# RWKV chunk products in four 64x64 quadrants of TensorE, and two preparation passes moved from VectorE to ScalarE

## Chip, cores, metric

One core of a Trainium2 chip runs one program. The metric is the device time in microseconds of one execution, the median of several.

## The reference, cut to what matters

Two layers; in each, a feed-forward half-step, a mixer of three branches on 512 tokens of 1024 features, a second feed-forward half-step and a gated embedding. The change touches only the RWKV branch: 8 heads of width 64, chunks of 64 tokens, all in float32. Per chunk and head it computes

```python
lhs = jnp.eye(RW_CHUNK, dtype=f32) - L_ab                    # unit lower triangular
W1 = triangular_solve(lhs, a_dec)
U0 = triangular_solve(lhs, L_ak @ v)
Q_eff = r_dec + M_rb @ W1
Y_intra = M_rb @ U0 + M_rk @ v
P = W1.T @ b_dec + exp(g_last) * eye(n)
D = U0.T @ b_dec + v.T @ k_dec
S_next = S @ P + D                                            # over the 8 chunks, in order
y = Y_intra + Q_eff @ S.T
```

before which the decays are cumulated and exponentiated, `kk = k * k_k` is divided by its norm over the head, and `k = k * (1 + (a - 1) * k_a)`.

## The kernel before

**Dense products.** Every large product runs through one helper (`open_group`, L848). Weights come by DMA on SP's queue into a ring of three slots; POOL splits each into a high and a low half (L1169, L1172), and TensorE multiplies three combinations of 128x128 by 128x512.

**The RWKV cores.** Heads are taken in pairs: core `ft` (0 to 3) handles two heads of 64 features, four token tiles of 128 tokens, each of two chunks (`cp` 0 and 1, in partitions 0 to 63 and 64 to 127). `rwkv_core_pe` issues for one core, in this order on TensorE: the pair products (L388), transposes to token-major (L379), then six levels that widen the inverse of `lhs` from blocks of 1 to 64. A level is the strips (L402), which VectorE masks into `xl` (L697), then the widening of `inv` (L414), which VectorE adds (L730), and that of `invT` (L420), which VectorE adds (L735). Each of these is 16 products of 64x64 by 64x64 and leaves 32 records, since a float32 product is two passes. Then the solution (L484, 16 products with 128 columns), which ScalarE copies to `xx` (L1581); the products for P and Q (L498, L502) and D (L508, L512), four passes of 16; the part of y inside the chunk (L524, L528); and a loop over chunks 1 to 7 that needs the previous state (L544, L550; VectorE adds at L750).

Between these, `advance(n)` issues n blocks of a dense product (three matmuls of 512 columns each): the numbers stand in `FILL_MANY` (cores 0 and 1), `FILL_FEW` (core 2) and `FILL_LAST` (core 3). PSUM banks come from `take`: the bank used longest ago, 3 to 7 for cores 0 and 1 and 4 to 7 for cores 2 and 3; TensorE waits there for the step that frees the bank's last user.

**VectorE and ScalarE.** Each has one instruction order, written out. While core `ft` runs, VectorE also prepares core `ft + 1`: `prepare_dve` is a generator, and `core_dve` takes steps from it by `aside(n)` at fixed places: one before the bonus, two after each strip of levels 2 to 5, two after each `invT` update, one before P and Q are added (L743), one per chunk of the state loop. From its step 12 on they are: `kk` (L590), the cumulation (L594), `rw_csm` (L597), the two operations on `k` (L604, L608), L613, the maximum of the key norms (L616), then L624, L626, L631, the scaling of `kk` by the inverse norm (L635), L639, L641, L644, L647, L652, L654. ScalarE's inverse norm is `norms_keys` (a table load, Ln at L1421, a table load, Exp at L1422); it stands in ScalarE's order behind the copies of D (L1585). `norm_squares` (L1393) and `decays` (L1399 to L1402) stand before the copy of the solution.

```python
            aside(1)

            now("rw_kept", L, ft)
            for cp in range(2):
                now("rwpq_done", L, ft, cp)
```

Of the kernel before, what the change touches and what calls it, by code (L numbers as in the profile page):

```python
# [28 lines left out]
P = 128  # L29
# [33 lines left out]
R_LNG, R_LNB, R_MU, R_W0, R_A0, R_KK, R_KA, R_RK, R_LB, R_HN, R_GNG, R_GNB = 0, 32, 64, 79, 83, 87, 91, 95, 99, 107, 111, 115  # L63
# [74 lines left out]
def build(nc, a, out, counts, banks_of):  # L138
# [4 lines left out]
    with ctx:  # L143
# [175 lines left out]

        def bank_units(b):  # L320
            return b[:, :].rearrange("p (u n) -> p u n", n=HEAD)
# [42 lines left out]
        def rwkv_core_pe(pe, take_bank, used_last, advance, L, ft):  # L364
# [3 lines left out]
            UNITS = [(hd, t) for t in range(NT) for hd in range(2)]  # L368
# [7 lines left out]
            def token_major(i, src):  # L376
                b = take(("rwt", L, ft, i), ("rw_tok", L, ft, i))
                for t in range(NT):
                    ins = nc.tensor.transpose(b[:, t * P:(t + 1) * P], src(t), ident())  # L379
                ins.then_inc(*step("rwt_done", L, ft, i))  # L380
# [11 lines left out]

            def strips(lev):
                b = take(("rwx", L, ft, lev), ("rw_x", L, ft, lev) if lev else ("rw_inv", L, ft, 0))
                if lev == 0:
                    for hd in range(2):
                        pe.wait_ge(*after("rw_mask", L, ft, 0, hd))
                else:
                    pe.wait_ge(*after("rw_inv", L, ft, lev - 1))
                for hd, t in UNITS:  # L400
                    for cp in range(2):
                        ins = nc.tensor.matmul(b[unit(cp), unit_cols(hd, t)], bm[unit(cp), hd, t, 0, :],  # L402
                                               ident()[unit(cp), unit(cp)] if lev == 0 else inv[unit(cp), NT * hd + t, :],
                                               start=True, stop=True)
                ins.then_inc(*step("rwx_done", L, ft, lev))

            def widen(lev):
                pe.wait_ge(*after("rw_x", L, ft, lev))
                pe.wait_ge(*after("rw_invT", L, ft, lev - 1))
                if lev < top:  # L410
                    b = take(("rwi", L, ft, lev), ("rw_inv", L, ft, lev))
                    for hd, t in UNITS:
                        for cp in range(2):
                            ins = nc.tensor.matmul(b[unit(cp), unit_cols(hd, t)], invT[unit(cp), NT * hd + t, :],  # L414
                                                   xl[unit(cp), NT * hd + t, :], start=True, stop=True)
                    ins.then_inc(*step("rwi_done", L, ft, lev))
                b = take(("rwj", L, ft, lev), ("rw_invT", L, ft, lev))
                for hd, t in UNITS:
                    for cp in range(2):
                        ins = nc.tensor.matmul(b[unit(cp), unit_cols(hd, t)], xl[unit(cp), NT * hd + t, :],  # L420
                                               invT[unit(cp), NT * hd + t, :], start=True, stop=True)
# [8 lines left out]
            strips(0)  # L430
# [3 lines left out]
            token_major(1, lambda t: ar[:, t, 0, :])  # L434
# [15 lines left out]
            for lev in range(2, top + 1):  # L450
# [4 lines left out]
                if lev == 2:  # L455
# [4 lines left out]
                    b = take(("rwl", L, ft), ("rw_lakv", L, ft))  # L460
                    for hd, t in UNITS:
                        for cp in range(2):
                            ins = nc.tensor.matmul(b[unit(cp), unit_cols(hd, t)], km[unit(cp), hd, t, 0, :],
                                                   v_tok[unit(cp), ft % 2, t, unit(hd)], start=True, stop=True)
# [12 lines left out]
            pe.wait_ge(*after("rw_lakv", L, ft))  # L477
            pe.wait_ge(*after("rw_tok", L, ft, 1))
            pe.wait_ge(*after("rw_invT", L, ft, top))
            for hd in range(2):  # L480
                b = take(("rwu", L, ft, hd), ("rw_wu", L, ft, hd))
                for t in range(NT):
                    for cp in range(2):
                        ins = nc.tensor.matmul(b[unit(cp), t * P:(t + 1) * P], invT[unit(cp), NT * hd + t, :], rhs[unit(cp), hd, t, :],  # L484
                                               start=True, stop=True)
                ins.then_inc(*step("rwu_done", L, ft, hd))
# [7 lines left out]
            for hd in range(2):  # L494
                pe.wait_ge(*after("rw_wu", L, ft, hd))
                for t in range(NT):
                    for cp in range(2):
                        nc.tensor.matmul(pq_bank[cp][unit(hd), t * HEAD:(t + 1) * HEAD], xx[unit(cp), hd, t, 0:HEAD],  # L498
                                         b_tok[unit(cp), t, unit(hd)], start=True, stop=True)
                for t in range(NT):  # L500
                    for cp in range(2):
                        ins = nc.tensor.matmul(pq_bank[cp][unit(hd), 256 + t * HEAD:256 + (t + 1) * HEAD], xx[unit(cp), hd, t, 0:HEAD],  # L502
                                               bm[unit(cp), hd, t, 1, :], start=True, stop=True)
                        if hd and t == NT - 1:
                            ins.then_inc(*step("rwpq_done", L, ft, cp))
                for t in range(NT):
                    for cp in range(2):
                        nc.tensor.matmul(d_bank[cp][unit(hd), t * HEAD:(t + 1) * HEAD], b_tok[unit(cp), t, unit(hd)],  # L508
                                         xx[unit(cp), hd, t, HEAD:P], start=t == 0, stop=False, skip_group_check=True)
                for t in range(NT):  # L510
                    for cp in range(2):
                        ins = nc.tensor.matmul(d_bank[cp][unit(hd), t * HEAD:(t + 1) * HEAD], k_tok[unit(cp), t, unit(hd)],  # L512
                                               v_tok[unit(cp), ft % 2, t, unit(hd)], start=False, stop=t == NT - 1,
                                               skip_group_check=True)
                        if hd and t == NT - 1:
                            ins.then_inc(*step("rwd_done", L, ft, cp))
# [51 lines left out]
        def prepare_dve(v, now, chain, L, ft):  # L568
# [21 lines left out]
            v.tensor_scalar(rw_kk[:, :], rkv[:, 1, :], parT[:, R_KK + ft:R_KK + ft + 1], None, ALU.mult).then_inc(*step("rw_kkr", L, ft))  # L590
            yield

# [14 lines left out]
            now("rw_made", L, ft, "ka")  # L607
            v.scalar_tensor_tensor(rw_k2[:, :], rw_k2[:, :], 1.0, rkv[:, 1, :], ALU.add, ALU.mult).then_inc(*step("rw_k2", L, ft))  # L608
# [606 lines left out]
        def _(act):  # L1215
# [174 lines left out]
            def norm_squares(L, ft):  # L1390

                now("rw_kkr", L, ft)
                nc.scalar.activation(rw_ss[:, :], rw_kk[:, :], ACT.Square).then_inc(*step("rw_sq", L, ft))  # L1393
# [616 lines left out]
```

## Time and profile before

| what | value |
|---|---|
| runs of before | 3162.68, 3166.0, 3166.46 us, median 3166.0 us |
| the profiled execution | 3162.28 us, its span 3160.2 us |
| mean granted TensorE clock | 0.984 |
| TensorE matmul busy | 3018.1 us (96%), 20178 records |
| VectorE busy | 1380.2 us (44%), 1779 instructions |
| ScalarE busy | 628.4 us (20%), 1023 instructions |
| GpSimd busy | 2350.3 us (74%), 1877 instructions |

Busy is the union of the instructions' times; a matmul's end is modelled and its records overlap, so the distance from one start to the next tells what a product costs. All times in rows are us from the span's start, unless ns is written. The eight cores run from 682.5 to about 891 us (layer 0) and from 2249.4 to about 2459 us (layer 1).

### The profile page before, as it was taken

How to read it: one execution, taken by the hardware profiler on the slowest of the kernel's cores; microseconds unless marked ns; L12 is line 12 of the kernel's file. 1: busy time of each engine (PE TensorE's matmuls, PEld its weight loads, DVE VectorE, ACT ScalarE, POOL GpSimd, SP SyncE). 2: the span in 40 equal slices, each digit the busy share in tenths (PEclk: the TensorE clock that was granted, in tenths of full speed). 3: DMA queues.
4: the chain of work that ended last, by engine and by line, in shares of the span. 5: the costliest groups of instructions: out<-in, count | busy, mean ns of one | idle time of the engine just before them, and what ended most of it. 6: DMA issues, size and time to landing. Idle time of an engine off the chain costs nothing. (4 is left out here: it accounts for less than half of the span.)

```text
span 3160.2 us, 47691 instructions
## 1 busy us (share of the span) xinstructions
PE 3018.1 (96%) x20178; PEld 2460.4 (78%) x20178; DVE 1380.2 (44%) x1779; ACT 628.4 (20%) x1023; POOL 2350.3 (74%) x1877
## 2 busy tenths in 40 slices
PE   8999999889989999999899999998999899999996
PEld 7888877677768888888788888776777688888884
DVE  4221333766636563211852214248665375622127
ACT  1000125443310020000310002354432100200011
POOL 8988786743249989888899888867331599898875
PEclk9999999999989999999999999999999899999998
DMA  4332332111013333323233223321110133333322
GB/s 138 100 100 94 100 120 61 43 44 39 29 41 94 126 95 106 100 94 100 87 94 107 94 100 107 105 57 47 40 46 16 54 94 126 100 107 94 100 87 87
DMA packets 201488, 266.60 MB, mean 84 GB/s; under 512 B 12305, under 2 KB 130429, under 8 KB 201277
## 3 DMA queue, kind: packets, MB, share of 16 engines
q1 hardware_dynamic: 194624, 243.51, 25.3%
q10 hardware_dynamic: 6652, 20.05, 1.7%
q8 instruction: 160, 2.62, 0.3%
q14 instruction: 52, 0.42, 0.0%
HBM read 257.22 MB, written 6.29 MB: 83 GB/s over the span
## 5 line engine op out<-in xcount | busy, mean ns | idle before, releaser
L1169 POOL TENSOR_TENSOR w_hi<-w_raw,zero 128x512 fp32r<-128x512 f32 (+2 forms) x936 | 1088.3, 1163 | 703.4 <-PE ps L848 661.8
L1172 POOL TENSOR_TENSOR w_lo<-w_raw,w_hi 128x512 fp32r<-128x512 f32 (+2 forms) x936 | 1288.5, 1377 | 73.5
L848 PE MATMUL ps<-hT_hi,w_hi 128*128 128x512 f32 (+1 forms) x2368 | 933.7, 394 | 35.7 <-DVE y_raw L793 15.6
L848 PE MATMUL ps<-hT_hi,w_lo 128*128 128x512 f32 (+1 forms) x2368 | 909.3, 384 | 0.0
L848 PE MATMUL ps<-hT_lo,w_hi 128*128 128x512 f32 (+1 forms) x2368 | 908.8, 384 | 0.0
L848 PEld LDWEIGHTS ps<-hT_hi,w_hi 128*128 128x128 f32 x2368 | 446.3, 188 | 148.2 <-POOL w_lo L1172 22.5
L848 PEld LDWEIGHTS ps<-hT_hi,w_lo 128*128 128x128 f32 x2368 | 445.7, 188 | 89.5
L848 PEld LDWEIGHTS ps<-hT_lo,w_hi 128*128 128x128 f32 x2368 | 446.9, 189 | 84.6 <-issue 2.9
L1723 DVE TENSOR_TENSOR act_raw<-silu,ps 128x512 f32<-128x512 f32 x88 | 59.9, 681 | 616.9 <-PE ps L848 616.9
L848 PE MATMUL ps<-w_hi,aT_hi 128*128 128x512 f32 x704 | 274.7, 390 | 0.0
L848 PE MATMUL ps<-w_lo,aT_hi 128*128 128x512 f32 x704 | 274.1, 389 | 0.0
L848 PE MATMUL ps<-w_hi,aT_lo 128*128 128x512 f32 x704 | 274.0, 389 | 0.0
L1312 ACT ACTIVATE silu<-ps 128x512 f32<-128x512 f32 x88 | 52.7, 598 | 883.6 <-PE ps L848 880.0
L1743 DVE SCALAR_TENSOR_TENSOR h_tok<-ps,h_tok 128x512 f32<-128x512 f32 x48 | 32.8, 683 | 437.3 <-PE ps L848 437.3
L848 PEld LDWEIGHTS ps<-w_lo,aT_hi 128*128 128x128 f32 x704 | 132.2, 188 | 27.5
L848 PEld LDWEIGHTS ps<-w_hi,aT_hi 128*128 128x128 f32 x704 | 132.2, 188 | 27.2
L848 PEld LDWEIGHTS ps<-w_hi,aT_lo 128*128 128x128 f32 x704 | 132.2, 188 | 27.2
L848 PE MATMUL ps<-w_hi,hT_hi 128*128 128x512 f32 x320 | 128.8, 402 | 3.4 <-POOL w_lo L1172 2.4
L1727 DVE TENSOR_TENSOR aT_lo<-act_raw,aT_hi 128x512 fp32r<-128x512 f32 x88 | 129.1, 1467 | 3.0
L848 PE MATMUL ps<-w_lo,hT_hi 128*128 128x512 f32 x320 | 124.9, 390 | 0.0
L848 PE MATMUL ps<-w_hi,hT_lo 128*128 128x512 f32 x320 | 124.8, 390 | 0.0
L1269 ACT ACTIVATE ln_rstd<-ln_mv,ln_eps 128x1 f32<-128x1 f32 x32 | 9.5, 297 | 441.6 <-DVE ln_mv L1686 441.6
(303 smaller groups left out, 3558.3 us busy)
## 6 DMA issues: line engine op xcount, KB each, us to landing
w_raw<-in_w_in SPq DMA_DIRECT2D x104, 512.0 KB, 3.6
w_raw<-in_ffn_wg SPq DMA_DIRECT2D x176, 256.0 KB, 2.8
w_raw<-in_ffn_wu SPq DMA_DIRECT2D x176, 256.0 KB, 3.1
w_raw<-in_ffn_wd SPq DMA_DIRECT2D x88, 512.0 KB, 3.6
w_raw<-in_w_in SPq DMA_DIRECT2D x96, 128.0 KB, 2.3
w_raw<-in_w_out SPq DMA_DIRECT2D x16, 512.0 KB, 3.8
w_raw<-in_ple_gate SPq DMA_DIRECT2D x16, 512.0 KB, 3.7
ln_rows<-in_ln_g ACTq DMA_DIRECT2D x8, 512.0 KB, 4.0
```

Source lines behind the costliest of these rows:

```text
L848: ins = nc.tensor.matmul(o, l_, r_, start=first, stop=last, skip_group_check=into is not None)
L1169: nc.gpsimd.tensor_tensor(w_split[0][:, q, kk, 0:w], w_raw[:, r, kk, 0:w], zero[:, 0:1].to_broadcast([P, w]), ALU.add).then_inc(*step("w_h ...
L1172: nc.gpsimd.tensor_tensor(w_split[1][:, q, kk, 0:w], w_raw[:, r, kk, 0:w], w_split[0][:, q, kk, 0:w].bitcast(F32), ALU.subtract).then_inc( ...
L1269: nc.scalar.activation(ln_rstd[:, t, :], ln_mv[:, t, 1:2], ACT.Sqrt, bias=ln_eps[:, :]).then_inc(*step("ln_sqrt", L, q, t))
L1312: nc.scalar.activation(silu[:, m, :], b[:, :], ACT.Silu).then_inc(*step("silu_done", L, f, g, m))
L1723: v.tensor_tensor(act_raw[:, m, :], silu[:, m, :], b[:, :], ALU.mult).then_inc(*step("act_raw", L, f, g, m))
L1727: v.tensor_tensor(aT[1][:, k, :], act_raw[:, m, :], aT[0][:, k, :].bitcast(F32), ALU.subtract).then_inc(*step("act_rest", L, f, k))
L1743: v.scalar_tensor_tensor(z, b[:, :], 0.5 if name == "down" else 1.0, z, ALU.mult, ALU.add).then_inc(*step("res_sum", L, q, half, m))
```

## The change

`PLACES` replaces `UNITS`: for odd token tiles the row half and the output half of a product differ (`side = cp ^ (t % 2)`), so that even tiles use the two quadrants on the diagonal and odd tiles the two others. Even and odd tiles write to two PSUM banks. `xl`, `invT` and the right-hand side of odd tiles lie in the other partition half than their chunk. This holds for the strips of levels 1 to 5, the widening of `inv`, the product of `km` with v and the solution. The widening of `invT` stays within halves. At level 0 the crossed copy of odd tiles is made by 8 more products into a bank of its own (`rwc`), and the transposes of `ar` for odd tiles become two products of 64 output partitions each. P, Q and D are reordered to `corners`, and both waits for `xx` now stand before them. VectorE's masks and additions on `xl` and `inv` are split in two by parity. `kk = k * k_k` is no longer made beforehand: ScalarE squares with a scale, and VectorE multiplies k by `k_k` where it scales by the inverse norm. `1 + (a - 1) * k_a` is made by one ScalarE instruction in `decays`. So two steps of `prepare_dve` fall away. The diff, cut:

```diff
+            PLACES = [(hd, t, cp, cp ^ (t % 2)) for hd in range(2) for t in range(NT) for cp in range(2)]
...
             def strips(lev):
-                b = take(("rwx", L, ft, lev), ("rw_x", L, ft, lev) if lev else ("rw_inv", L, ft, 0))
...
+                b = two_banks("rwx", "rw_x", lev)
+                pe.wait_ge(*after("rw_inv", L, ft, lev - 1, 1))
+                for hd, t, cp, side in PLACES:
+                    ins = nc.tensor.matmul(b[t % 2][unit(side), parity_cols(hd, t)], bm[unit(cp), hd, t, 0, :],
+                                           inv[unit(cp), NT * hd + t, :], start=True, stop=True)
...
             def widen(lev):
...
+                    b = two_banks("rwi", "rw_inv", lev)
+                    for hd, t, cp, side in PLACES:
+                        ins = nc.tensor.matmul(b[t % 2][unit(cp), parity_cols(hd, t)], invT[unit(side), NT * hd + t, :],
+                                               xl[unit(side), NT * hd + t, :], start=True, stop=True)
...
+                for hd, t, cp, side in PLACES:
+                    u = NT * hd + t
+                    ins = nc.tensor.matmul(b[unit(cp), HEAD * u:HEAD * u + HEAD], xl[unit(cp), u, :], invT[unit(cp), u, :],
+                                           start=True, stop=True)
...
+            b = [take(("rwu", L, ft, odd), ("rw_wu", L, ft, odd)) for odd in range(2)]
+            last = {}
+            for hd, t, cp, side in PLACES:
+                c = P * (2 * hd + t // 2)
+                last[t % 2] = nc.tensor.matmul(b[t % 2][unit(cp), c:c + P], invT[unit(side), NT * hd + t, :],
+                                               rhs[unit(side), hd, t, :], start=True, stop=True)
+            for odd in range(2):
+                last[odd].then_inc(*step("rwu_done", L, ft, odd))
...
+            for odd in range(2):
+                pe.wait_ge(*after("rw_wu", L, ft, odd))
+            corners = ((0, 0), (1, 1), (0, 1), (1, 0))
+            for t in range(NT):
+                for cp, hd in corners:
+                    nc.tensor.matmul(pq_bank[cp][unit(hd), t * HEAD:(t + 1) * HEAD], xx[unit(cp), hd, t, 0:HEAD],
+                                     b_tok[unit(cp), t, unit(hd)], start=True, stop=True)
...
-            v.tensor_scalar(rw_kk[:, :], rkv[:, 1, :], parT[:, R_KK + ft:R_KK + ft + 1], None, ALU.mult).then_inc(*step("rw_kkr", L, ft))
-            yield
...
-            now("rw_a", L, ft)
-            now("rw_csm", L, ft)
+            now("rw_ka", L, ft)
             if ft:
                 now("rwb_done", L, ft - 1)
-            v.tensor_scalar(rw_k2[:, :], rw_a[:, :], 1.0, parT[:, R_KA + ft:R_KA + ft + 1], ALU.subtract, ALU.mult).then_inc(
-                *step("rw_made", L, ft, "ka"))
-            yield
...
-            v.scalar_tensor_tensor(rw_kk[:, :], rw_kk[:, :], SS_SCALE ** 0.5, rw_ss[:, :], ALU.mult, ALU.mult).then_inc(
+            v.scalar_tensor_tensor(rw_kk[:, :], rkv[:, 1, :], parT[:, R_KKS + ft:R_KKS + ft + 1], rw_ss[:, :], ALU.mult, ALU.mult).then_inc(
...
+                nc.scalar.activation(rw_ss[:, :], rkv[:, 1, :], ACT.Square, scale=parT[:, R_KK + ft:R_KK + ft + 1]).then_inc(*step("rw_sq", L, ft))
...
             def decays(L, ft):
                 now("rw_csm", L, ft)
+                now("par_more", L)
+                nc.scalar.activation(rw_k2[:, :], rw_a[:, :], ACT.Identity, bias=parT[:, R_KA1 + ft:R_KA1 + ft + 1],
+                                     scale=parT[:, R_KA + ft:R_KA + ft + 1]).then_inc(*step("rw_ka", L, ft))
```

The `aside` counts stay as they are, so every later step of `prepare_dve` moves to a place two earlier. On VectorE, in core 1 of a layer, from the last strips to the first state, before:

```order
L697 TENSOR_TENSOR xl<-ps,cons 128x8x32 [waits rwx_done]
L608 SCALAR_TENSOR_TENSOR rw_sw<-rw_sw,rkv 128x512 [waits rw_made]
L613 TENSOR_TENSOR rw_keep<-rkv,rw_sw 128x512 [waits rw_k2]
L735 TENSOR_TENSOR invT<-invT,ps 128x8x32 [waits rw_invT,rwj_done]
L616 TENSOR_SCALAR rw_ss<-ps 128x512 [waits rwss_done]
L624 TENSOR_TENSOR ar<-rkv,rw_e 128x4x128 [waits rwm_done,rwt_done,rw_e3]
L626 TENSOR_TENSOR k_inv<-rw_sw,rw_cs 128x512
L743 TENSOR_TENSOR pq<-ps,pq_add 128x8x64 [waits rwpq_done,rw_kept]
L743 TENSOR_TENSOR pq<-ps,pq_add 128x8x64 [waits rwpq_done]
L750 TENSOR_TENSOR rhs<-ps,rhs 128x64 [waits rws_done,rw_d]
```

and now:

```order
L717 TENSOR_TENSOR xl<-ps,cons 128x4x32 [waits rwx_done]
L717 TENSOR_TENSOR xl<-ps,cons 128x4x32
L635 TENSOR_SCALAR rw_ss<-ps 128x512 [waits rwss_done]
L643 TENSOR_TENSOR ar<-rkv,rw_e 128x4x128 [waits rwm_done,rwt_done,rw_e3]
L760 TENSOR_TENSOR invT<-invT,ps 128x8x32 [waits rw_invT,rwj_done]
L645 TENSOR_TENSOR k_inv<-rw_sw,rw_cs 128x512
L650 TENSOR_TENSOR rw_dec<-k_inv,rw_e 128x512 [waits rw_made]
L654 SCALAR_TENSOR_TENSOR rw_kk<-rkv,parT,rw_ss 128x512 [waits rw_rn]
L768 TENSOR_TENSOR pq<-ps,pq_add 128x8x64 [waits rwpq_done,rw_kept]
L768 TENSOR_TENSOR pq<-ps,pq_add 128x8x64 [waits rwpq_done]
L775 TENSOR_TENSOR rhs<-ps,rhs 128x64 [waits rws_done,rw_d]
```

The maximum of the key norms now stands ahead of the last `invT` update, and the scaling of `kk`, which waits for ScalarE's `rw_rn`, ahead of both additions of P and Q; before, both stood behind.

On TensorE in the changed kernel, core 1, from P to the part of y inside the chunk (it is L498 to L528 of the kernel before, and waits there for the same two names):

```order
L525 MATMUL ps<-b_tok,xx 64x64 x15
L529 MATMUL ps<-bm,xx 64x64 x16
L535 MATMUL ps<-xx,b_tok 64x64 x16
L539 MATMUL ps<-v_tok,k_tok 64x64 x16
L551 MATMUL ps<-xx,bm 64x64 [waits rw_pq,rw_wu]
L551 MATMUL ps<-xx,bm 64x64 x7
```

The part of y waits for `rw_pq` because `take` gives it the bank from which VectorE adds P and Q.

On VectorE in the changed kernel, before core 0, from the end of the cumulation on:

```order
L621 TENSOR_TENSOR rw_e<-rw_cs,rw_sw 128x512 [waits rw_made]
L627 TENSOR_TENSOR rw_sw<-rw_sw,rkv 128x512 [waits rw_ka]
L1953 TENSOR_TENSOR y_raw<-ps,hg_g 128x512 [waits hg_in,hg_osq]
L632 TENSOR_TENSOR rw_keep<-rkv,rw_sw 128x512 [waits hgo_done,rw_k2]
L1953 TENSOR_TENSOR y_raw<-ps,hg_g 128x512 [waits hg_in,hg_osq]
L635 TENSOR_SCALAR rw_ss<-ps 128x512 [waits rwss_done]
L1953 TENSOR_TENSOR y_raw<-ps,hg_g 128x512 [waits hg_in,hg_osq]
L643 TENSOR_TENSOR ar<-rkv,rw_e 128x4x128 [waits rw_e3]
L1953 TENSOR_TENSOR y_raw<-ps,hg_g 128x512 [waits hg_in,hg_osq]
```

Before, all four products of the HGRN branch (L1918) stood ahead of the maximum of the key norms; now two of them stand behind it.

## Rows read from the trace of the kernel before

**Rows 1.** Page, busy time of each engine: TensorE.

```profile
PE 3018.1 (96%) x20178; PEld 2460.4 (78%) x20178; DVE 1380.2 (44%) x1779; ACT 628.4 (20%) x1023; POOL 2350.3 (74%) x1877
```

**Rows 2.** Windows: start:end, length, busy time (and instructions) of each engine, granted clock, DMA.

```profile
2249.40:2361.60 112.20, 111.16 (x1920) 87.37 (x1920) 69.99 (x127) 43.08 (x72) 33.00 (x28) 0.98 0.12 32
```

**Rows 3.** Timeline of TensorE, core 1 of layer 1: start, us, line, what, [idle before].

```profile
2315.48 1.10 PE L402 MATMUL ps<-inv,bm 64*64 64x64 f32 x32
2316.41 1.10 PE L463 MATMUL ps<-v_tok,km 64*64 64x64 f32 x32
```

**Rows 4.** Groups by line and form: strips; busy us, mean ns, idle before.

```profile
L402 PE MATMUL ps<-inv,bm 64*64 64x64 f32 x1280 | 44.5, 219 | 3.6 <-DVE inv L711 3.0 <-DVE inv L730 0.5
```

**Rows 5.** Timeline of TensorE: pair products in four quadrants, 128 columns.

```profile
2305.25 1.10 PE L388 MATMUL ps<-ar,b_inv 64*64 64x128 f32 x32
2306.29 1.21 PE L379 MATMUL ps<-cons,rw_dec 128*128 128x128 f32 x8
```

**Rows 6.** Timeline of TensorE, core 0 of layer 1: where L512 and L498 meet.

```profile
2290.89 0.22 PE L498 MATMUL ps<-b_tok,xx 64*64 64x64 f32 x1
2290.90 0.22 PE L512 MATMUL ps<-v_tok,k_tok 64*64 64x64 f32 x1
2290.90 0.22 PE L498 MATMUL ps<-b_tok,xx 64*64 64x64 f32 x1
2290.95 0.22 PE L512 MATMUL ps<-v_tok,k_tok 64*64 64x64 f32 x1
```

**Rows 7.** Timeline of TensorE, core 1 of layer 1: from the solution to y.

```profile
2341.57 1.97 PE L484 MATMUL ps<-rhs,invT 64*64 64x128 f32 x32
2343.47 0.50 PE L848 MATMUL ps<-hT_hi,w_hi 128*128 128x512 f32 x1
...
2345.06 0.68 PE L498 MATMUL ps<-b_tok,xx 64*64 64x64 f32 x16
...
2348.84 0.68 PE L524 MATMUL ps<-xx,bm 64*64 64x64 f32 x16
...
2350.85 0.50 PE L848 MATMUL ps<-hT_hi,w_hi 128*128 128x512 f32 x1
```

**Rows 8.** Timeline of ScalarE, the same stretch.

```profile
2342.71 0.60 ACT L1581 ACTIVATE xx<-ps 128x512 f32<-128x512 f32 x1 [5.38 <-PE ps L484]
...
2348.87 0.66 ACT L1585 ACTIVATE rhs<-ps 128x256 f32<-128x256 f32 x2 [4.68 <-PE ps L512]
...
2352.78 0.63 ACT L1422 ACTIVATE rw_ss<-rw_ss 128x512 f32<-128x512 f32 x1
```

**Rows 9.** Timeline of VectorE, core 1 of layer 1.

```profile
2314.76 0.42 DVE L730 TENSOR_TENSOR inv<-inv,ps 128x256 f32<-128x256 f32 x1 [0.40 <-PE ps L414]
...
2340.29 0.69 DVE L616 TENSOR_SCALAR rw_ss<-ps 128x512 f32<-128x512 f32 x1 [0.62 <-PE ps L348]
...
2348.00 1.29 DVE L743 TENSOR_TENSOR pq<-ps,pq_add 128x512 f32<-128x512 f32 x2 [4.98 <-PE ps L502]
...
2354.24 1.28 DVE L635 SCALAR_TENSOR_TENSOR rw_kk<-rw_kk,rw_ss 128x512 f32<-128x512 f32 x1
```

**Rows 10.** Timeline of TensorE: waits before core 0 and in core 2, layer 1.

```profile
2249.40 0.92 PE L388 MATMUL ps<-ar,b_inv 64*64 64x128 f32 x12 [6.39 <-issue]
...
2363.65 0.55 PE L379 MATMUL ps<-cons,rw_dec 128*128 128x128 f32 x3 [0.86 <-DVE yt L765]
...
2403.45 0.68 PE L524 MATMUL ps<-xx,bm 64*64 64x64 f32 x15 [0.60 <-DVE pq L743]
```

**Rows 11.** Windows behind the wait before core 0, columns as in rows 2.

```profile
2249.40:2253.10 3.70, 3.70 (x41) 3.37 (x42) 2.62 (x6) 0.60 (x1) 0.00 (x0) 0.50 0.34 96
...
2253.20:2257.00 3.80, 3.79 (x100) 3.13 (x99) 2.11 (x4) 0.60 (x1) 0.00 (x0) 1.00 0.02 4
```

**Rows 12.** Timelines before and in core 0: VectorE, ScalarE.

```profile
2233.08 0.69 DVE L1918 TENSOR_TENSOR y_raw<-ps,hg_g 128x512 f32<-128x512 f32 x1 [0.41 <-ACT y_raw L1544]
...
2279.67 1.27 ACT L1416 ACTIVATE y_raw<-ps,parT 128x512 f32<-128x512 f32 x2 [4.26 <-PE ps L447]
```

More of the change, by code:

```diff
@@ L391, in pairs, with two_banks @@
                     last[hd].then_inc(*step("rwm_done", L, ft, i, hd))
-            def strips(lev):
-                b = take(("rwx", L, ft, lev), ("rw_x", L, ft, lev) if lev else ("rw_inv", L, ft, 0))
[L395 to L404, printed above, removed]
+            def two_banks(name, freed, lev):
+                return [take((name, L, ft, lev, odd), (freed, L, ft, lev, odd)) for odd in range(2)]
@@ new lines, in first_strips @@
+            def first_strips():
+                b = take(("rwx", L, ft, 0, 0), ("rw_inv", L, ft, 0, 1))
+                b2 = take(("rwc", L, ft), ("rw_invT", L, ft, 0))
+                for hd in range(2):
+                    pe.wait_ge(*after("rw_mask", L, ft, 0, hd))
+                for hd, t, cp, side in PLACES:
+                    eye = ident()[unit(cp), unit(cp)]
+                    u = HEAD * (NT * hd + t)
+                    ins = nc.tensor.matmul(b[unit(cp), u:u + HEAD], bm[unit(cp), hd, t, 0, :], eye, start=True, stop=True)
+                    if t % 2:
+                        ins = nc.tensor.matmul(b2[unit(side), parity_cols(hd, t)], eye, bm[unit(cp), hd, t, 0, :],
+                                               start=True, stop=True)
+                ins.then_inc(*step("rwx_done", L, ft, 0))
@@ L429, in rwkv_core_pe @@
             advance(fill["pairs"])
-            strips(0)
+            first_strips()
             pairs(1, k_inv)
@@ L459, in rwkv_core_pe @@
                     pe.wait_ge(*after("rw_tok", L, ft, 0))
[L460 to L464, printed above, removed]
+                    b = two_banks("rwl", "rw_lakv", 0)
+                    for hd, t, cp, side in PLACES:
+                        ins = nc.tensor.matmul(b[t % 2][unit(side), parity_cols(hd, t)], km[unit(cp), hd, t, 0, :],
+                                               v_tok[unit(cp), ft % 2, t, unit(hd)], start=True, stop=True)
                     ins.then_inc(*step("rwl_done", L, ft))
@@ L475, in rwkv_core_pe @@
             advance(fill["last"])
-            pe.wait_ge(*after("rw_lakv", L, ft))
+            pe.wait_ge(*after("rw_lakv", L, ft, 0, 1))
             pe.wait_ge(*after("rw_tok", L, ft, 1))
             pe.wait_ge(*after("rw_invT", L, ft, top))
[L480 to L486, printed above, removed]
+            b = [take(("rwu", L, ft, odd), ("rw_wu", L, ft, odd)) for odd in range(2)]
+            last = {}
+            for hd, t, cp, side in PLACES:
+                c = P * (2 * hd + t // 2)
[3 more added lines that the diff above has]
+                last[odd].then_inc(*step("rwu_done", L, ft, odd))
             advance(fill["solve"])
@@ L493, in rwkv_core_pe @@
             d_bank = [take(("rwd", L, ft, cp), ("rw_d", L, ft, cp)) for cp in range(2)]
[L494 to L516, printed above, removed]
@@ L520, in rwkv_core_pe @@
+            for cp in range(2):
+                last[cp].then_inc(*step("rwd_done", L, ft, cp))
             y_bank = [take(("rwy", L, ft, hd), ("rw_y2", L, ft, hd)) for hd in range(2)]
@@ L727, in core_dve @@
                     now("rwi_done", L, ft, lev)
-                    now("rw_inv", L, ft, lev - 1)
-                    early = of_units(inv[:, :, :], hgt, 0)
-                    v.tensor_tensor(early, early, of_units(bank_units(bank("rwi", L, ft, lev)), hgt, 0), ALU.add).then_inc(
-                        *step("rw_inv", L, ft, lev))
+                    now("rw_inv", L, ft, lev - 1, 1)
+                    for odd in range(2):
+                        early = of_units(of_parity(inv[:, :, :], odd), hgt, 0)
+                        v.tensor_tensor(early, early, of_units(bank_parity(bank("rwi", L, ft, lev, odd)), hgt, 0), ALU.add).then_inc(
+                            *step("rw_inv", L, ft, lev, odd))
                 now("rwj_done", L, ft, lev)
```

93 lines of the change are left out of this document (60 added, 33 removed).

## Prediction, on record before the changed kernel ran

> **What bounds the kernel now.** The page's busy times come first: TensorE is busy for 3018.1 of 3160.2 us, VectorE for 44%, ScalarE for 20% [rows 1]. The windows show the same inside core 0 of layer 1: 111.16 of 112.20 us [rows 2]. So a product that goes costs its spacing, and a wait on TensorE counts in full. The timeline gives spacings: one step's first start to the next's, since the modelled ends overlap. Strips start at 2315.48 and the products behind them at 2316.41: 0.93 us for 32 records, 29 ns each, on two quadrants [rows 3]. The mean of 219 ns in the groups by form is latency, no cost [rows 4]. The other waits that matter are three: 6.39 us ahead of core 0, 0.86 between cores 1 and 2, and 0.60 ahead of y in core 2, whose bank VectorE's pq addition still holds [rows 10].
>
> **What becomes shorter.** On four quadrants with 64 columns no row shows sustained work. The nearest: 128 columns on four quadrants take 1.04 us for 32 records, a switch included, at most 33 and about 27 ns each without it [rows 5]. But where P's and D's products meet, of other quadrants each, four starts lie within 0.01 us, the fourth being L512's at 2290.95 after a pause of 0.05 [rows 6]. The lower bound is half of 29, 14.6 ns (the row's 0.93 by 32, halved); the upper is 27. I take 14.6: it is the same operation at the same width. The other end is the second rival. Per core: five strips save 0.46 each, four widenings of inv 0.46 each, the product of km with v 0.46; the solution goes from 1.90 (2341.57 to 2343.47) to about 1.03, and P, Q and D from 3.78 (2345.06 to 2348.84) to about 1.9 [rows 7]. Sum: 2.30 + 1.85 + 0.46 + 0.87 + 1.90 = 7.4 us, in eight cores **-59 us**.
>
> The Trainium skill ("TensorE: Matmul & The Clock Gate", section "Wait — 56ns, not 53.3ns?") says that start-to-start never falls below about 25 ns, however few the columns. The starts in [rows 6] lie closer than that, but for a few records only; by the rule each of the 448 records a core would save about 4 ns, 14 us in all, and the sum would give 3217, near the second rival.
>
> **What becomes longer or waits.**
>
> Crossed transposes: 16 products of half height in place of 8, 0.25 us a core by the spacing of [rows 3]: **+2**.
>
> Scaling of kk. This is the largest cost. VectorE's step L654 needs ScalarE's inverse norm, and ScalarE makes it behind its copies of D: these start at 2348.87 and the last Exp ends at 2353.41, so 4.57 us after D's end at 2348.84, two table loads in it [rows 7, 8]. In the changed order L654 stands ahead of the pq additions, and the part of y waits for one of them through its bank. So y starts at D's end + 4.57 + the scaling, 0.69 (as L616 alone; L635 with 1.28 ran beside other work) + one addition of 0.65 + two handovers, about 0.3: 6.2 us, where cores 0 and 1 now wait for nothing and core 2 for 0.60 [rows 9, 10]. What is queued behind it on TensorE is y, its fill and the whole state loop, so nothing covers it. Core 3 prepares no other core. 6 cores by 6.2: **+37** (by the 0.60 of core 2 the bounds are 5.6 and, with 1.28, 6.9 a core).
>
> Clock. Behind the 6.39 us wait before core 0 the granted clock is 0.50, the lower of the two levels, for 3.7 us of full activity, and then 1.00 again [rows 10, 11]. So half of 3.7 is lost, 1.85; I take 2.2, since the return may be later. Bounds 0 and 3.7 a wait. Six such waits: **+13**.
>
> Last invT update. It now stands behind the norms' maximum and ar, 0.69 each [rows 9]; part lies beside the fill. I take 0.45 in cores 0 and 1 and 1.15 in core 2, which has one fill block less; bounds 0 and 1.4: **+4**.
>
> Copies of xx. In before the first copy ran beside the second half of the solution (2342.71, ahead of the end at 2343.47) [rows 7, 8]. Now both start at its end and need 1.2 with handovers around. Two fill blocks (1.59 to 2345.06) cover that in cores 0 and 1; one in cores 2 and 3 doesn't: 0.8 by four cores, **+3** (bounds 0, and 1.2 each).
>
> Start of core 0. VectorE's k now needs ScalarE's ka, which stands behind work of the other branch there: 1.5 by two layers, **+3**; the two ScalarE copies of 1.27 that stand together [rows 12] bound it at 0 and 2.5. Two y_raw products of 0.69 move behind the maximum of the norms, inside the stretch that ends the 6.39 us wait: 1.3 by two, **+2.6** (0 to 1.4).
>
> Banks. Each level takes two, so a bank comes round sooner. The transposes before core inverse wait for the mask of the first products (0.2 in cores 0 and 1, 0.6 in 2 and 3: +3.2); core 2's last bank waits for VectorE's copies, 0.9 by two: +1.8. Together **+5**, bounds 0 and 10.
>
> Handover to the next core. Two steps of the preparation are gone, so its last step ends sooner. The wait of 0.86 goes and the fill around the others shrinks with it: about 2.4 a layer, **-4.7** (0 to -7).
>
> ScalarE takes up two passes of 0.6 a core; it is busy for 20% and nobody but core 0 waits. Cost nothing; without the cover 0.6 a core. The splits on VectorE (two operations where 0.42 did for one [rows 9]) end about 0.75 us behind the products, and the widening of invT, 0.93, lies beside them: nothing, and the third rival if not. No DMA moves.
>
> Sum: -59 + 2 + 37 + 13 + 4 + 3 + 3 + 2.6 + 5 - 4.7 = **+6 us**. The profiled execution has 3162.28 us (span 3160.2) and would come to about 3168.7; it lies 3.7 under the median of the runs, 3166.0, so the time I give is 3172. A difference under 0.2%, 6.3 us, is about what a measurement of this kernel can't tell from none.
>
> **Rivals.**
>
> *The clock holds.* The waits of about 6 us may not lower the clock, as each has matmuls at full rate ahead of it, where the wait before core 0 had other idle time near. Then the 13 us are gone: 3159. For: each wait is a little shorter than the 6.39. Against: that one does show 0.50 [rows 11]. It decides whether the result is faster.
>
> *No gain from the other quadrants.* If starts stay about 27 ns apart, the lowest sustained row [rows 5], 448 records a core (strips 160, inv 128, km with v 32, P, Q and D 128) save 2 ns each, 7 us in eight cores in place of 59. That is 52 on top of 3172: 3224. Slower, decided by the spacing of the 32 records of strips: over 22 ns the change loses. For: the only long row. Against: it has twice the columns, and [rows 6].
>
> *VectorE bounds the levels.* With products at half their time a level has 0.46 us less to cover masks and additions, and each mask is two operations. If each of nine waits a core grows by 0.3 us, eight cores give 20 us more: 3192. For: VectorE ends inv only at 2315.18 and TensorE's strips start at 2315.48 [rows 3, 9], so no slack. Against: I have placed the wait behind a product of 0.93 that stays.
>
> That the change doesn't do what it says (the order on TensorE puts one quadrant's products behind the same quadrant's) would be seen as the second rival and gives its time.
>
> **How the numbers follow.** The sum as worked out 0.48, its own range 3164 to 3180 and to either side by its unknown bounds: faster 0.05, same 0.20, slower 0.23. Clock holds 0.24, 3159: faster 0.16, same 0.08, the sum's spread around it. No gain 0.14: slower. VectorE bounds 0.14: slower, but for 0.01 same. That is faster 0.21, same 0.29, slower 0.50. The range takes in the first two and the last, 3150 to 3195, and leaves out the rival at 3224 and the ends of the bounds.
>
> **What would show it.** Right: strips and widening of inv start 0.47 us apart for 32 records in the timeline of TensorE; P to D's end 1.9 us in place of 3.78; in the timeline, y in cores 0 to 2 idle for about 6 us behind VectorE's pq, while VectorE's L654 waits for ScalarE's Exp; in the windows behind it a granted clock of 0.50; solution's copies late in cores 2 and 3; 7 to 8 us idle ahead of core 0. Wrong: spacing near 25 ns; a clock of 1.00 behind these waits; idle times of TensorE ended by VectorE's L717 or L756 at each level; or y behind D at once, which would mean that the inverse norm is early and the change faster by 50.

## Result and profile after

| | before | changed |
|---|---|---|
| median of runs | 3164.9 us (5 runs, 3161.7 to 3166.5) | 3178.9 us (5 runs, 3173.9 to 3182.7) |
| profiled execution | 3162.28, span 3160.2 | 3173.90, span 3171.8 |
| granted clock, mean | 0.984 | 0.979 |

Ratio 1.0045, 95% interval 1.0034 to 1.0057: slower by 14 us, where 3172 was forecast. The page's busy times of the changed kernel, to be read against [rows 1]:

```profile
PE 2976.6 (94%) x20354; PEld 2412.3 (76%) x20354; DVE 1381.9 (44%) x1847; ACT 636.4 (20%) x1039; POOL 2359.1 (74%) x1877
```

TensorE works for 41.5 us less (3018.1 to 2976.6), with 176 records more, and the span is 11.6 us longer. The products became shorter and the waits ate more than that. The timeline of TensorE, core 1 of layer 1 of the changed kernel (start, us, line, what, idle before), shows both:

```profile
2334.15 0.69 PE L440 MATMUL ps<-xl,invT 64*64 64x64 f32 x32
2334.66 1.10 PE L446 MATMUL ps<-invT,xl 64*64 64x64 f32 x32
2335.55 0.68 PE L430 MATMUL ps<-inv,bm 64*64 64x64 f32 x32
...
2341.26 0.69 PE L430 MATMUL ps<-inv,bm 64*64 64x64 f32 x32 [1.22 <-DVE inv L755]
...
2351.98 0.65 PE L535 MATMUL ps<-xx,b_tok 64*64 64x64 f32 x32
2352.44 0.65 PE L539 MATMUL ps<-v_tok,k_tok 64*64 64x64 f32 x32
2359.22 1.12 PE L551 MATMUL ps<-xx,bm 64*64 64x64 f32 x16 [6.13 <-DVE pq L768]
```

A float32 product of 64x64 leaves two records here (16 issued, x32 in the row). 32 records in four quadrants take 0.46 us (2351.98 to 2352.44) to 0.51 (L440, a switch of quadrants and tiles included), 14.4 to 16 ns each; the widening of invT, still on two, takes 0.89. In [rows 3] it was 0.93 for the strips. Strips with a dense block behind them take 0.61 to the block's start, where they took 1.03 before. Ahead of y stand 6.13 us of idle time. VectorE and ScalarE in the same place:

```profile
2357.72 0.75 DVE L654 SCALAR_TENSOR_TENSOR rw_kk<-rkv,parT,rw_ss 128x512 f32<-128x512 f32 x1 [6.74 <-ACT rw_ss L1452]
2358.38 1.28 DVE L768 TENSOR_TENSOR pq<-ps,pq_add 128x512 f32<-128x512 f32 x2
```

```profile
2353.14 0.66 ACT L1617 ACTIVATE rhs<-ps 128x256 f32<-128x256 f32 x2 [2.55 <-PE ps L539]
2353.82 1.28 ACT L1451 ACT_TABLE_LOAD   x1
...
2357.05 0.63 ACT L1452 ACTIVATE rw_ss<-rw_ss 128x512 f32<-128x512 f32 x1
```

D ends, ScalarE copies it, makes the inverse norm in 3.9 us, and only then VectorE scales kk and adds P and Q: the chain that the prediction drew from [rows 7 to 9]. The windows give the clock of the first 3.4 us of y in core 0 (columns as in rows 2):

```profile
2299.50:2302.90 3.40, 3.37 (x63) 3.40 (x64) 0.48 (x1) 0.00 (x0) 0.00 (x0) 0.50 0.02 5
```

To sum it up, the stages of the eight cores, each from the first start of one step to the first start of the next in TensorE's timeline (before, change, and the experiment that stands first below):

| stage, sum over eight cores, us | forecast | changed - before | e1_places - before | changed - e1_places |
|---|---|---|---|---|
| pairs to first widening | +1.5 | +0.7 | +7.0 | -6.2 |
| first widening to km with v | -7.4 | -6.1 | -6.2 | +0.1 |
| km with v to solution | -19.9 | -7.7 | -21.3 | +13.6 |
| solution to P | -3.8 | -4.6 | -4.5 | -0.1 |
| P to y | +22.0 | +23.3 | -13.3 | +36.6 |
| y to next core (six) | +8.5 | +10.7 | +2.7 | +8.0 |
| sum | +0.9 | +16.2 | -35.8 | +52.0 |

The forecast column is the prediction's terms put where they act (for km with v to the solution, seven groups of 0.46 by eight and the terms for invT and core 2's bank). Outside of the cores the span changed by 11.6 - 16.2 = -4.6 us. That is mostly the stretch from y of the last core of layer 0 to the first pair products of layer 1, for the most part dense products that the change does not touch (1364.5 us before, 1359.7 changed). It took 1359.7 to 1365.5 over the profiled executions here, and 1360.0 and 1365.5 in two experiments (e11 and e12) whose code differs there only in y and its transposes. So it is taken as variation and not as an effect of the change.

### The profile page after: what moved, and what is told of

The parts are those of the page before. It is cut to its first block and busy times, and to the rows that moved or that the text cites. A ratio compares the mean times of both kernels' runs of the same rounds, so it can differ in the third digit from the quotient of the medians.

```text
span 3171.8 us, 48189 instructions
## 1 busy us (share of the span) xinstructions
PE 2976.6 (94%) x20354; PEld 2412.3 (76%) x20354; DVE 1381.9 (44%) x1847; ACT 636.4 (20%) x1039; POOL 2359.1 (74%) x1877
```

## Experiments

Theory A: the two steps that left VectorE's preparation pulled all later ones two places ahead, and that alone costs the time. Theory B: the split masks and doubled banks cost it inside the levels.

**e1_places.** The changed kernel, with an empty step where each of the two stood:

```diff
+            yield
             now("rw_sw", L, ft)
             v.tensor_tensor_scan(rw_cs[:, :], ...
...
+            yield
             now("rw_ka", L, ft)
```

> The changed kernel with an empty step of the preparation in the two places from which kk and the subtraction of a left, so that every later step stands where it stood before the change. Theory A (the two missing steps pulled the later ones ahead, and that alone costs the time): the wait of 6.34 us ahead of y goes in cores 0 to 2 of both layers (38 us), the lower clock behind it too (about 11 us), and the waits inside the levels with it (15 to 20 us): 3110 to 3118. Theory B (the waits inside the levels come from the split masks and additions and from two banks a level): only 49 us go, about 3130. Theory C (the quadrants themselves bring less than their spacing): above 3140.

Measured: 3126.8 us, 0.988 of before [0.9865, 0.9894], 52 us under the changed kernel. The wait ahead of y is gone in all six cores, the waits inside the levels mostly. Theory C is out. The waits that A named went, but 3127 lies outside its stretch and between A's and B's numbers, so this run alone does not decide between them; e3 does. In the table the levels give 13.6 us back where A said 15 to 20, but the first stage gives 6.2 away. In this kernel VectorE has no time to spare from the end of one core to the next, which the long idle ahead of y had hidden. VectorE at the start of core 2 in e1_places, and TensorE's weight loads (PEld), which stand first in the queue there:

```profile
2335.95 0.88 DVE L787 TENSOR_REDUCE gn_st<-ps 128x4 f32<-128x256 f32 x2
2336.87 0.17 DVE L788 TENSOR_SCALAR gn_st<-gn_st 128x8 f32<-128x8 f32 x1
2337.07 0.76 DVE L792 TENSOR_TENSOR yt<-ps,gn_st 128x256 f32<-128x256 f32 x2
2337.74 1.35 DVE L686 COPY_PREDICATED bm<-cons,ps 128x512 f32<-128x512 int32 x2
```

```profile
2337.55 0.43 PEld L394 LDWEIGHTS ps<-cons,rw_dec 128*128 128x128 f32 x4 [0.51 <-DVE yt L792]
...
2339.21 0.17 PEld L420 LDWEIGHTS ps<-cons,bm 64*64 64x64 f32 x2 [0.74 <-DVE bm L686]
```

No idle time stands in VectorE's rows, and TensorE waits twice for what comes out of them: 1.25 us, about what this core's first stage is longer than in the changed kernel (1.3).

**e2_kk_behind.** The changed kernel; one step moves from ahead of the additions of P and Q to behind them:

```diff
-            aside(1)
             now("rw_kept", L, ft)
...
+            aside(1)
             for c in range(1, NC - 1):
```

> The changed kernel with one step moved: the last step before the additions of P and Q, the scaling of kk, stands behind them and ahead of the state loop. Theory A: the 6.34 us ahead of y go in six cores (38 us) and the lower clock too (11), but the first addition of the state loop now waits for the scaling, 1 to 2 us a core; the waits inside the levels stay: 3132 to 3142. Theory B gives the same here. If the clock stays low because of the new wait, 5 to 10 us more.

Measured: 3139.9 us, 0.9923 [0.9902, 0.9943]: inside the expected stretch. Moving one instruction behind the two additions is worth 39 us. The 13.6 us inside the levels stay, as expected.

**e3_kk_ahead.** As e1_places, but with two more steps ahead of the additions:

```diff
-            aside(1)
+            aside(3)
             now("rw_kept", L, ft)
```

> As e1_places, but two more steps are taken ahead of the additions of P and Q, so that the scaling of kk stands ahead of them again. Theory A: the waits inside the levels are gone and the wait ahead of y is there: e1_places plus 49, near 3160, 15 to 20 below the changed kernel. Theory B: no better than the changed kernel, near 3179.

Measured: 3163.4 us, 0.9994 [0.9985, 1.0003], near A's 3160 and not B's 3179. The scaling ahead of the additions costs 36.6 us net in this pair (3163.4 - 3126.8), not 49: the idle time and the clock cost 44.5 in the stages, and 6.4 come back at the starts of the cores, since VectorE catches up while TensorE stands. And 15.4 us of the changed kernel (3178.9 - 3163.4) are the steps pulled into the levels: with the split masks and the doubled banks kept, that stage is 13.6 us shorter. B falls for these.

**e4_quadrants_only.** The changed kernel with kk and the subtraction of a back on VectorE:

```diff
+            v.tensor_scalar(rw_kk[:, :], rkv[:, 1, :], parT[:, R_KK + ft:R_KK + ft + 1], None, ALU.mult).then_inc(*step("rw_kkr", L, ft))
+            yield
...
-                nc.scalar.activation(rw_k2[:, :], rw_a[:, :], ACT.Identity, bias=parT[:, R_KA1 + ft:R_KA1 + ft + 1],
```

> The changed kernel with kk and the subtraction of a back on VectorE as two steps (the quadrants alone). Theory A: all places are as before the change, so within 5 us of e1_places, 3110 to 3120: the two passes on ScalarE are worth next to nothing by themselves. Rival: VectorE's two steps of 0.4 to 1.3 us lengthen the levels now that TensorE is quicker there, 10 us or more above e1_places.

Measured: 3133.3 us, 0.9897 [0.9882, 0.9912]. Both expectations missed: it is outside A's 3110 to 3120, and 6 above e1_places where the rival had 10 or more. The quadrants alone win 32 us; the passes on ScalarE are worth about 6 more when places are kept. In the profiles 3.1 us of this is in the cores, 2.4 of it inside core 1's levels. The intervals overlap, so 6 is a middle value and not clear of noise.

**e5_passes_only.** The kernel before with the passes moved and no quadrants (the same lines the other way round, on the kernel before):

```diff
-            v.tensor_scalar(rw_kk[:, :], rkv[:, 1, :], parT[:, R_KK + ft:R_KK + ft + 1], None, ALU.mult).then_inc(*step("rw_kkr", L, ft))
-            yield
...
+                nc.scalar.activation(rw_k2[:, :], rw_a[:, :], ACT.Identity, bias=parT[:, R_KA1 + ft:R_KA1 + ft + 1],
```

> The kernel before with the two passes on ScalarE alone: kk and the subtraction of a leave VectorE, the later steps move two places ahead, no quadrants. Theory A (the missing steps' places cost the time, whatever the products do): a wait of about 6.3 us ahead of y in six cores (38) and the lower clock (11), less about 6 at the starts of the next cores: kernel before plus 40 to 50, 3205 to 3216. Rival: with products at the old length there is enough cover, and it costs under 15.

Measured: 3214.5 us, 1.0155 [1.0142, 1.0169]: 50 us slower, at the upper end of the expected stretch. P to y is 6.10 longer in each of the six cores, y to the next core 11.2 in all, and the levels 10.2, which the expectation had no term for. The same waits stand in its timeline of TensorE, core 0:

```profile
2311.23 1.15 PE L420 MATMUL ps<-invT,xl 64*64 64x64 f32 x32 [1.41 <-DVE xl L689]
2315.36 1.96 PE L484 MATMUL ps<-rhs,invT 64*64 64x128 f32 x32 [0.53 <-DVE invT L727]
2328.71 1.12 PE L524 MATMUL ps<-xx,bm 64*64 64x64 f32 x16 [6.10 <-DVE pq L735]
```

So the cost belongs to the part of the change that takes work away from VectorE. It needs no quadrants.

**e7_pqd_as_before.** As e1_places, P, Q and D in the old order (all of one head, then all of the other, which uses two quadrants at a time):

```diff
-            corners = ((0, 0), (1, 1), (0, 1), (1, 0))
-            for t in range(NT):
-                for cp, hd in corners:
+            for hd in range(2):
+                for t in range(NT):
+                    for cp in range(2):
```

> As e1_places, with P, Q and D again in the order of before: 128 records a core at 29 ns in place of 14.6. If each record on the path costs its spacing: 1.66 us a core as measured between P and y, 13 us: 3138 to 3142. Rival (what the products save there comes back as a wait for VectorE or at the start of the next core): under 7, below 3134.

Measured: 3139.4 us, 0.9917 [0.9904, 0.993]: 12.5 us more than e1_places for 13.3 in the stage from P to y. On this piece a record costs its spacing. But in the profiled executions 2.9 of the 13.3 are given back from y to the next core, all in cores 0 and 1, where that stage is again as long as before the change. So part of what the quadrants win in P, Q and D was lost just behind them: in e1_places TensorE stands idle once inside y in each of these four cores, for 0.17 to 0.73 us, in e7 in none. What holds it there was not traced.

**e8_y_quadrants.** As e1_places, with y on four quadrants:

```diff
-                        nc.tensor.matmul(y_bank[hd][unit(cp), t * HEAD:(t + 1) * HEAD], bm[unit(cp), hd, t, 1, :],
+                        hd = cp ^ part
+                        nc.tensor.matmul(y_bank[hd][unit(cp ^ (t % 2)), t * HEAD:(t + 1) * HEAD], bm[unit(cp), hd, t, 1, :],
```

> As e1_places, with the part of y inside the chunk on four quadrants too: rows of odd tiles change halves, the transposes of y put them back, and one wait of TensorE for its own first half is added. If the spacing halves: 0.93 us less a core, 7.4 in eight, about 1.5 back for the wait and the transposes: 3119 to 3123. Rival: the first state product then comes before VectorE's Q and ScalarE's D are ready, and nothing is won in core 2 and 3: 3124 to 3127.

Measured: 3131.7 us, 0.9899 [0.9886, 0.9912]. No gain, if anything a loss of 5 (the intervals overlap; in the profiled executions the cores sum to the same): a miss. The stages say where it went: y to next core gives 3.6 us, and km with v to solution takes 3.7, 0.6 to 0.8 in cores 1 to 3 of both layers. That is the extra transposes, 1.04 us a core in place of 0.42, which the expectation put at too little. The groups by line of e12_y_and_norm, which has the same products:

```profile
L370 PE MATMUL ps<-cons,yt 128*128 128x64 f32 x64 | 8.5, 262 | 0.0
...
L559 PE MATMUL ps<-xx,bm 64*64 64x64 f32 x256 | 7.9, 229 | 3.7 <-DVE pq L781 1.8 <-issue 1.1
...
L373 PE MATMUL ps<-cons,yt 128*128 128x128 f32 x16 | 4.7, 296 | 0.0
```

A transpose leaves one record, the product that replaces it two per half: 64 for 16 transposes.

**e9_filled_wait.** The changed kernel, with products into the bank that is free during the wait ahead of y, cores 0 and 1:

```diff
-            y_bank = [take(("rwy", L, ft, hd), ("rw_y2", L, ft, hd)) for hd in range(2)]
+            y_bank = [take(("rwy", L, ft, 0), ("rw_y2", L, ft, 0))]
+            if ft < 2:
+                for _ in range(5):
+                    nc.tensor.matmul(y_bank[0][:, :], ident(), cons[:, 0:4, :].rearrange("p a n -> p (a n)"), start=True, stop=True)
+            y_bank.append(take(("rwy", L, ft, 1), ("rw_y2", L, ft, 1)))
```

> The changed kernel with five products of 128x512 on a free bank inside the wait ahead of y, in cores 0 and 1 of both layers; their results are overwritten. If the lower clock behind the waits costs what I take from the stages (y 1.5 us longer, the fill behind it 0.5): 2.0 less in four cores, 8 us: 3169 to 3173, and a granted clock of 1.00 in y. Rival (the clock is no cost of its own, what is lost behind y are other waits): no difference, 3177 to 3181.

Measured: 3179.0 us, 1.0047 [1.0033, 1.006], six runs from 3172.1 to 3186.9: no difference to the changed kernel in the median, against the expectation. That is the rival's number, but not its reason. The windows of its profile, of the slowest of the six runs, show both sides, y of core 1 and then core 2, which has no fill:

```profile
2309.10:2312.50 3.40, 3.40 (x72) 2.79 (x69) 0.19 (x1) 0.00 (x0) 0.00 (x0) 1.00 0.00 0
```

```profile
2414.00:2445.00 31.00, 23.85 (x300) 17.11 (x300) 9.15 (x22) 6.01 (x9) 2.05 (x2) 0.56 0.07 19
```

In the four filled cores the clock stayed at 1.00 and y to the next core became 2.07, 1.38, 2.08 and 1.39 us shorter, 1.7 in the mean. But behind the wait of core 2 in layer 1 the clock stayed at its lower level for most of 31 us, and that stage took 4.8 us more; in layer 0 core 2 lost 2.9. So the clock's price per wait is shown, what decides how long it stays low behind the next wait is open, and with it whether the longer stages of core 2 belong to the fill or to that one execution. The price goes with how far the lower level reaches into the work. In the changed kernel TensorE is busy at 0.50 for 4.72 us behind the start of y in core 0 and for 3.06 in core 1:

```profile
2299.53:2304.25 4.72, 4.72 (x67) 4.41 (x68) 0.45 (x1) 0.00 (x0) 0.00 (x0) 0.50 0.01 3
```

```profile
2359.22:2362.28 3.06, 3.06 (x58) 3.06 (x60) 0.45 (x1) 0.00 (x0) 0.00 (x0) 0.50 0.02 5
```

Half of that is 2.36 and 1.53, near the 2.08 and 1.39 that the filled cores give back in this layer.

**e10_one_ahead and e11_norm_early.** Theory D: in e1_places VectorE is late from y to the first masks. e10 changes

```diff
-            aside(1)
+            aside(2)
             now("rw_kept", L, ft)
```

and e11 adds:

```diff
+                    if ft < 3:
+                        norms_keys(L, ft + 1)
                     for cp in range(2):
                         now("rwd_done", L, ft, cp)
...
-                    if ft < 3:
-                        norms_keys(L, ft + 1)
```

```diff
+            aside(2)
             for cp in range(2):
                 now("rw_d", L, ft, cp)
```

the latter between the additions of P and Q and the state loop.

> As e1_places, with one more step of the preparation (the decay of k, 0.68 us, which waits for nothing of ScalarE's late work) ahead of the additions of P and Q, where VectorE stood idle for about 5 us before. Theory D (in e1_places VectorE is behind from the end of one core to the first masks of the next, which is why the first levels are 0.7 to 1.0 us longer than before the change): up to 0.7 us less in six cores, 3122 to 3126. Rival (those waits are of banks or of ScalarE's copies): the same as e1_places, 3125 to 3129.

> As e10, and ScalarE makes the inverse norm between the copies of the solution and those of D (it was idle for 4.68 us there before the change), so that VectorE can scale kk and make b between the additions of P and Q and the state loop. Theory D: three steps less behind the state loop, the extra time at the starts of six cores gone: 3117 to 3123. Rival: D's copies come 2.4 us behind D's end and the state loop waits for them, most in core 2 with one block of fill: no gain or a loss, 3126 to 3135.

Measured: e10 3124.2 us, 0.9876 [0.986, 0.9893]; e11 3119.5 us, 0.9858 [0.9843, 0.9872], the fastest of all, 45 under before and 59 under the changed kernel. e10's interval overlaps with that of e1_places, so its median decides nothing; in its stages core 3 starts 1.24 us sooner in both layers and core 2 as late as before. D holds by e11: in e11's stage from the pairs to the first widening cores 2 and 3 are at 9.40 us, as in the changed kernel, where e1_places had 10.6 to 10.7. ScalarE of e11, core 1 of layer 1:

```profile
2311.66 1.09 ACT L1615 ACTIVATE xx<-ps 128x512 f32<-128x512 f32 x2 [1.95 <-PE ps L509]
2312.76 1.28 ACT L1454 ACT_TABLE_LOAD   x1
...
2316.00 0.63 ACT L1455 ACTIVATE rw_ss<-rw_ss 128x512 f32<-128x512 f32 x1
2316.53 0.64 ACT L1622 ACTIVATE rhs<-ps 128x256 f32<-128x256 f32 x2
```

The norm fills what was idle time, D's copies follow at once, and VectorE scales kk at 2316.66, 3.37 us ahead of the state loop's first addition (2320.03).

**e12_y_and_norm.** e11 with e8's y.

> As e11_norm_early, with y on four quadrants as in e8_y_quadrants. In e8 the 0.6 to 1.4 us that y gave came back inside the levels and at the state loop. Theory D (VectorE bounds what lies behind y, and e11 has taken three steps off it there): now part of the 7.4 us stays, 3112 to 3117. Rival (the state loop waits for VectorE's and ScalarE's work on P, Q and D, which does not get earlier): the same as e11_norm_early, 3117 to 3122.

Measured: 3121.3 us, 0.9875 [0.9862, 0.9889]: the rival's stretch, though not by its reason. The three other steps made no room, since what y saves (2.8 us) goes to the transposes (3.5 us again, by stages). Before ran faster in this batch (median 3162.3, against 3164.6 in that of e11), and by the ratios e12 lies 5 us above e11, as e8 above e1_places.

**e13_norm_early_before.** The kernel before with e11's moves alone.

> The kernel before with only the moves of e11_norm_early: the inverse norm ahead of D's copies on ScalarE, one more step of the preparation ahead of the additions of P and Q and two behind them. No quadrants, no passes moved to ScalarE. Theory D: VectorE was nearly in time there (waits of 0.86 and less at the starts), so at most 1 to 3 us less: 3161 to 3165. Rival (the order on ScalarE was worth as much before as after the change): 3157 to 3160.

Measured: 3158.4 us, 0.9989 [0.998, 0.9998], 11 runs against 15 of before with a median of 3162.3: 4 us, a little more than expected and inside the rival's stretch. In the stages cores 2 and 3 start 1.3 to 1.4 us sooner (5.5 in the four, 5.1 over all eight). The expectation went by the waits named in the timeline (0.86 and less, [rows 10]). VectorE was late there already, D holds in kind, and its size in the kernel before was put too low.

## Why the prediction was right, and where it was not

**Spacing on four quadrants.** Right: 14.4 to 16 ns a record, over long runs of 32. The second rival (27 ns) fell. The Trainium skill's floor of about 25 ns ("TensorE: Matmul & The Clock Gate", section "Wait — 56ns, not 53.3ns?") does not hold for products that go to different quadrants: the trace has them at 14.4. (In [rows 6] three starts lie within 0.01 us, not four; the fourth comes 0.05 later.) Solution 1.03 us (forecast 1.03), P to D's end 1.9. To the start of y it is 2.12 in e1_places, so 1.66 less than before where 1.88 was forecast.

**Scaling of kk.** Right in chain and size: 6.2 us a core forecast; P to y is 6.10 longer than in e1_places in each of the six. e2 takes it away, e3 and e5 make it again.

**Clock.** Right that it falls, which disposes of the first rival: 0.50 in y. The term was 2.2 a wait, 13 in all. e9 gives 2.1 in core 0 and 1.4 in core 1, and core 2's was not measured by itself (its stage grew by 2.1 to 2.2): about 11 in all. 1.85, half of the 3.7 us in [rows 11], would have been nearer to the mean of 1.7 in e9.

**Last invT update, and the term that was missing.** "It now stands behind the norms' maximum and ar ... I take 0.45 in cores 0 and 1 and 1.15 in core 2", +4 in all. That wait came at about its size. It stands ahead of the solution, in cores 1 and 2 of layer 1 as

```profile
2348.38 1.10 PE L509 MATMUL ps<-rhs,invT 64*64 64x128 f32 x32 [0.49 <-issue]
...
2407.16 1.10 PE L509 MATMUL ps<-rhs,invT 64*64 64x128 f32 x32 [1.71 <-issue]
```

and sums to 5.4 us over the six cores. But the moved steps cost 13.6 us between km with v and the solution (changed less e1_places), about 2.1 in cores 0 and 1 and 2.6 in core 2. For the other 8 the sum had no term: this is the step that failed. The prediction followed the moved steps at two places, the last update and the additions of P and Q. It left out the ones before them, inside the levels. VectorE of the changed kernel, core 1, level 4:

```profile
2338.02 1.37 DVE L618 TENSOR_TENSOR_SCAN rw_cs<-starts,rw_sw 128x512 f32<-128x512 f32 x1
2339.42 1.30 DVE L621 TENSOR_TENSOR rw_e<-rw_cs,rw_sw 128x512 f32<-128x512 f32 x1
2340.65 0.47 DVE L755 TENSOR_TENSOR inv<-inv,ps 128x128 f32<-128x128 f32 x2
```

The subtraction of 1.30 us (L621), which stood behind both additions of that level (to inv and invT), now stands ahead of them, and TensorE waits 1.22 at 2341.26. In core 0 the masks of level 5 are late by 1.47 in the same way:

```profile
2284.61 1.15 PE L446 MATMUL ps<-invT,xl 64*64 64x64 f32 x32 [1.47 <-DVE xl L717]
```

**VectorE bounds the levels (third rival).** It came in part and is most of what was missed: not 0.3 us at nine waits a core, but one or two waits of over a microsecond where a step was pulled in. With the places kept, 4.5 us of 25.8 forecast there (seven groups of 0.46 in eight cores) are still missing, in cores 0, 2 and 3; core 1 gives 0.4 more than forecast. The waits in e1_places there are 0.34 for L719 and 0.26 for L757 in core 0, 0.34 for L719 and 0.19 for ScalarE's rw_sw in core 2, and 0.31 for L820 in core 3. A smaller part is that strips ahead of a dense block save 0.42 and not 0.46.

**Banks and starts.** Forecast +5 for banks and -4.7 for handovers. The changed kernel shows +0.7 in its first stage for +1.5 forecast, but VectorE had caught up in the wait ahead of y. In e1_places it is +7.0. I put the loss down to banks; most of it is VectorE, since e10 and e11 take 3.8 and 5.6 off. Of the handovers little came in the stage where the table puts them: in e9, where the clock stays up, y to the next core is as before the change in core 0 and 0.27 less in core 1. So +10.7 for +8.5 is a clock term put too high and a handover term that hardly came.

**Copies of xx.** Forecast +3.2, measured 2.4 (solution to P, -4.6 against -7.0 for the products): right.

**Before core 0.** Forecast +5.6 for the two layers. The wait ahead of core 0 is 6.9 us in the changed kernel; two sum to 13.8 in its groups by line, where two of 6.39 [rows 10] make 12.8: +1.0. The wait for ScalarE's ka did come, and it is long:

```profile
2237.53 1.08 DVE L627 TENSOR_TENSOR rw_sw<-rw_sw,rkv 128x512 f32<-128x512 f32 x1 [9.66 <-ACT rw_sw L1425]
```

But VectorE had idle time there before, 5.08 us ahead of the maximum of the norms, and now has 1.43, so most of the delay never reached TensorE. The prediction priced the wait and not the idle time that covers it. With the places kept (e1_places) the two waits of TensorE sum to 13.2, so about 0.4 of the 1.0 goes with ka and 0.6 with the moved steps.

```profile
L403 PE MATMUL ps<-ar,b_inv 64*64 64x128 f32 x256 | 10.6, 312 | 13.8 <-issue 13.8
```

**The total.** In the profiled executions +11.6 where +6.4 was forecast: 15.3 more inside the cores (12.2 of them between km with v and the solution), 10.2 less outside (-4.6 for +5.6). The 12.2 are about 8 for the steps inside the levels, 1.4 for the last update, 4.5 for what is missing with the places kept, less the 1.8 of core 2's bank, which did not come. The medians moved by +14. The mechanism, products shorter by half and a wait of 6 us with a lower clock behind it, was right. That the time lies this near to 3172 is partly luck: two errors of opposite sign met, and the -4.6 outside is mostly variation that nobody forecast.

## To carry to other kernels

Where one engine's order is written as a stream of side steps dealt out at fixed places, taking a step out is a change of the order of all later ones: keep its place empty, or deal anew. Follow every moved step to the instruction that now stands behind it, not only those next to a known wait. When an engine becomes idle for microseconds it also hides what others are late with, so an undo brings less than the wait and the clock behind it cost (36.6 for 44.5 here), and the next late engine has to be sought again.

## What the runs showed of the hardware

64x64 products of float32 that go round four quadrants start every 14.4 to 16 ns per record over runs of 32, half of the 29 on two quadrants. After an idle time of 6 us TensorE's granted clock is 0.50; with five products of 128x512 in that time it stays at 1.00 and the stage behind is 1.4 to 2.1 us shorter, about half of the time that TensorE worked at 0.50. A table load on ScalarE takes 1.28 us, and the pair of Ln and Exp with a load each 3.9. In one profiled execution the clock stayed low for most of 31 us with 23.85 of them busy, which nothing here explains.
